# Loading x in four column parts between the first weight units, and the first norm's vector apart from the others

## The chip, the core and the metric

One Trainium2 chip (trn2), one core. The metric is the device time of the whole program in microseconds (us): the median of three executions before the change is 1454.51 us (1451.9 to 1456.7).

## The reference, cut to what matters

One decoder layer on 256 tokens of width 2048, all in f32. What the change touches is the very first step:

```python
h = rms_norm(x, norm_mix[l])
proj = h @ w_in[l]              # columns: q-latent 512 | kv-latent 256 + rope key 64 | SB q, k, v 3 x 1024
# ... MLA attention (softmax, rotary), stick-breaking attention
x = x + concat(rms_norm(o_mla), rms_norm(o_sb)) @ w_out[l]
x = x + memory_cross_attention(rms_norm(x), rms_norm(mem), ...)
x = x + hierarchical_moe(rms_norm(x), ...)   # 32 experts, f32 weights of 12 MB each
y = rms_norm(x)
```

`rms_norm(x, g)` is `x * rsqrt(mean(x*x) + eps) * g`. The kernel multiplies by `g` before the projection and by the factor of each row (the rsqrt) after it, when the accumulated bank is copied out.

## The kernel before, in words

Every engine has one program of its own, run in order, and they meet through semaphores only.

**Weights.** The projections are cut into chunks of 512 output columns (`Q_LAT` = 0, `KV_LAT` = 1 with 320 columns, then `SB_Q`, ...), and each chunk into units of 256 input rows: 8 units for a chunk over D = 2048, 512 KB a unit. `SyncE` (SP) loads unit `u` into slot `u % 4` of the ring `w_raw` (line 312), once `w_split` says that the unit four places back was split (line 304). `ScalarE` (ACT) rounds it to `w_hi` (`rounded`, line 772), which also waits until TensorE has used the unit that held the slot (`w_used`, line 771). `VectorE` (DVE) forms the rest `w_lo = w_raw - w_hi` (`split_w`, line 1066). TensorE (PE) then does twelve matmuls for the unit (lines 408 to 410).

**Activations.** `split_turn` (line 388) transposes x on PE, two 128-column blocks (index k) at a time into one bank of PSUM. ACT makes `a_hi` with the gain as scale (`split_head`, line 798, scale from `g_t`), DVE makes `a_lo` (`split_rest`, line 1077). For the first norm these steps are interleaved with the units: `split_project` on PE (pair kk is turned, then unit kk - 3 is multiplied), `heads_and_units` on ACT, `rests_and_units` on DVE. The 8 pairs use 4 banks of PSUM in turn.

**The start.** SP loads x in two DMAs of 128 rows and waits for both before it issues the first weight unit (lines 299 to 301). ACT issues eight small DMAs of the norm vectors into `g_nat`, two of the positions and one of `g_ffn` (lines 833 to 842), then loads its table. PE waits for the constants and all eight vectors, transposes `g_nat` once (line 448), ACT copies the result to `g_t` (line 845), and PE waits for that copy before it turns x. DVE first computes the rotary angles (lines 1128 to 1149), then begins `rests_and_units`. GpSimd (POOL) writes the inverse frequencies, the identity and the masks.

**The end of the first norm.** ACT, after `heads_and_units("mix")`, squares x for the row factors (`squares_of`, line 778), waits for POOL's pow (`rstd`, lines 1586 and 1587), and only then comes to

```python
            for c in range(Q_LAT, Q_PE):
                rounded(UNIT0[c + 1] + RING)
```

so that units 8 to 11, the first of chunk `KV_LAT`, are rounded behind it. PE comes to `KV_LAT` with `project(c)` right after `split_project`.

After the projections come the attentions, w_out, the attention into memory, the router, and a loop over 32 experts whose weights SP streams from HBM; the first expert's weights are issued when PE has used the units up to `MEM_O` (line 335).

Of the kernel before, what the change touches and what calls it, by code (L numbers as in the profile page):

```python
# [20 lines left out]
ALU = mybir.AluOpType  # L21
ACT = mybir.ActivationFunctionType
AX = mybir.AxisListType.X

P = 128
# [16 lines left out]
SC_SB = float(HD) ** -0.5  # L42
BLK = 3 * P
RING = 4
UK = 2
UN = 512

# [40 lines left out]
def layer(nc, x, mem, positions, norm_mix, w_in, norm_q_lat, w_q_b, norm_kv_lat, w_kv_b,  # L88
# [11 lines left out]
    with ctx:  # L100
# [195 lines left out]

        @block.sync
        def _(sp):
            for t in range(TT):
                sp.dma_start(x_res[:, t, :], x[0, t * P:(t + 1) * P, :]).then_inc(S("x_loaded"), 16)  # L300
            sp.wait_ge(S("x_loaded"), 16 * TT)
            for u, (c, i) in enumerate(UNITS):
                if u >= RING:
                    sp.wait_ge(S("w_split"), u - RING + 1)
                dst = w_raw[:, u % RING, :, 0:chunk_cols(c)]
                (src,) = unit_src(c, i)
                if len(src.shape) == 4:
                    for k in range(UK):
                        sp.dma_start(dst[:, k, :].rearrange("p (h c) -> p h c", h=src.shape[2]),
                                     src[:, k]).then_inc(S(f"w_loaded{u % RING}"), 16)  # L310
                else:
                    sp.dma_start(dst, src).then_inc(S(f"w_loaded{u % RING}"), 16)

            def load_gate_up(e, side, used=None, halves=(0, 1)):

                wg = w_gate[0, e].rearrange("(p k) f -> p (k f)", k=KD)
                wu = w_up[0, e].rearrange("(p k) f -> p (k f)", k=KD)
                half = KD // 2 * FE
                for b in halves:
                    if used is not None:  # L320
                        sp.wait_ge(S(f"gu_used{b}"), used)
                    for m, w in enumerate((wg, wu)):
                        sp.dma_start(gu[side][:, b, m].rearrange("p k f -> p (k f)"),  # L323
                                     w[:, b * half:(b + 1) * half]).then_inc(
                                         S(f"gu_loaded{side}{b}"), 16)

            def load_down(e, used=None):
                wd = w_down[0, e].rearrange("(j p) d -> p j d", p=P)
                for b, dst in enumerate((down0, down1)):
                    if used is not None:  # L330
                        sp.wait_ge(S(f"down_used{b}"), used)
                    sp.dma_start(dst[:, :, :], wd[:, 2 * b:2 * b + 2, :]).then_inc(
                        S(f"down_loaded{b}"), 16)

            sp.wait_ge(S("w_used"), UNIT0[MEM_O])
            sp.wait_ge(S("mem_scores"), MEM_HEADS)

            load_gate_up(0, 0)
            load_down(0)
            sp.wait_ge(S("w_used"), len(UNITS))  # L340
            sp.wait_ge(S("w_split"), len(UNITS))
            load_gate_up(1, 1)
            for e in range(2, AHEAD):
                load_gate_up(e, e % 2, e - 1)
                load_down(e - 1, e - 1)
            load_gate_up(AHEAD, AHEAD % 2, AHEAD - 1, halves=(0,))
            load_down(AHEAD - 1, AHEAD - 1)
            load_gate_up(AHEAD, AHEAD % 2, AHEAD - 1, halves=(1,))
            load_down(AHEAD, AHEAD)
            with sp.Fori(0, (EXPERTS - AHEAD - 1) // 2) as i:  # L350
                for m in range(2):
                    e = 2 * i + AHEAD + 1 + m
                    load_gate_up(e, (AHEAD + 1 + m) % 2, 2 * i + AHEAD + m)
                    load_down(e, 2 * i + AHEAD + 1 + m)
            sp.wait_ge(S("routed"), 1)
            total = sp.value_load(n_iter[0:1, 0:1], min_val=EXPERTS, max_val=MAX_PASSES * EXPERTS)
            with sp.If(total > EXPERTS):

                with sp.Fori(EXPERTS - 1, total - 1, EXPERTS) as before_:
                    with sp.Fori(0, EXPERTS // 2) as i:  # L360
                        for side in range(2):
                            load_gate_up(2 * i + side, side, before_ + 2 * i + side)
                            load_down(2 * i + side, before_ + 2 * i + 1 + side)
            sp.wait_ge(S("gu_used1"), total)
            sp.dma_start(g_fin[:, :], norm_final.rearrange("(a d) -> a d", a=1).to_broadcast([P, D])
                         ).then_inc(S("final_gain_loaded"), 16)
            for t in range(TT):
                for f in range(2):
                    sp.wait_ge(S("final"), 2 * t + f + 1)
                    cols = slice(f * D // 2, (f + 1) * D // 2)  # L370
                    sp.dma_start(out[0, t * P:(t + 1) * P, cols], x_res[:, t, cols]).then_inc(
                        S("stored"), 16)
            sp.wait_ge(S("stored"), 16 * 2 * TT)
# [3 lines left out]
        def _(pe):  # L377
            def split_turn(name, src, k_from=0, k_to=None):

                k0, kn = SPLIT0[name], SPLIT_K[name]  # L380
                for kk in range(k_from // 2, (kn if k_to is None else k_to) // 2):
                    b = k0 // 2 + kk
                    if b >= 4:
                        pe.wait_ge(S("split_lo"), 2 * (b - 4) + 2)
                    for i in range(2):
                        for t in range(TT):
                            k = 2 * kk + i
                            mm = pe.transpose(ps[4 + b % 4][:, i * SEQ + t * P:i * SEQ + (t + 1) * P],  # L388
                                              src[:, t, k * P:(k + 1) * P], ident[:, :])
# [37 lines left out]
            def turn(c):  # L427
# [6 lines left out]
                for b in range(1 if c == KV_LAT else 2):  # L434
# [8 lines left out]
                                              nat[:, j % 2, t, f * P:(f + 1) * P], ident[:, :])  # L443
                    mm.then_inc(S("turned"), 1)

            pe.wait_ge(S("consts"), 1)
            pe.wait_ge(S("gains_loaded"), 8 * 16)
            pe.transpose(ps[0][:, 0:86], g_nat[:, :], ident[0:86, 0:86]).then_inc(S("gains_turned"), 1)
            pe.wait_ge(S("x_loaded"), 16 * TT)
            pe.wait_ge(S("gains_copied"), 1)  # L450
            split_project("mix", x_res, [(Q_LAT, i, 0) for i in range(KD // UK)])
            for c in range(Q_LAT, Q_PE):
                if c > Q_LAT:
                    project(c)
                if SB_Q <= c - 1 < SB_V:
                    turn(c - 1)
# [302 lines left out]
        def _(sc):  # L759
# [70 lines left out]

            xsq = [0]

            for gain, r0, rows in ((norm_mix, 0, 16), (norm_mem_src, 16, 16), (norm_mem_x, 32, 16),
                                   (norm_q_lat, 48, 4), (norm_kv_lat, 52, 2), (norm_mla_out, 54, 8),
                                   (norm_sb_out, 62, 8), (norm_ffn, 70, 16)):
                sc.dma_start(g_nat[r0:r0 + rows, :], gain[0].rearrange("(k p) -> k p", p=P)
                             ).then_inc(S("gains_loaded"), 16)
            for t in range(TT):
                sc.dma_start(pos_i[:, t:t + 1], positions[0, t * P:(t + 1) * P].rearrange(
                    "(p a) -> p a", a=1)).then_inc(S("pos_loaded"), 16)  # L840
            sc.dma_start(g_ffn[:, :], norm_ffn[0].rearrange("(p k) -> p k", k=KD)).then_inc(
                S("ffn_gain_loaded"), 16)
            sc.preload_act_table_set("natural_log_exp_and_others")
            sc.wait_ge(S("gains_turned"), 1)
            sc.activation(g_t[:, :], ps[0][:, 0:86], ACT.Copy).then_inc(S("gains_copied"), 1)
            sc.wait_ge(S("gains_copied"), 1)
            heads_and_units("mix", 0, 0)
            junk = v_mla[:, :, :].rearrange("p t d -> p (t d)")
            squares_of(x_res, SS_X, junk)
            sc.wait_ge(S("rstd"), 1)  # L850
# [200 lines left out]
        def _(ve):  # L1051
# [68 lines left out]
            rt_a = place("rope_tmp", [P, 4, 256], offset=e_at + 80 * 1024)  # L1120


            from math import pi
            import numpy as np
            half = ROPE // 2
# [16 lines left out]
            for cc in (c1, c2, c3):  # L1142
# [4 lines left out]
            link(ve.tensor_tensor(cosv, cosv, turns[:, :, :], ALU.add))  # L1147
            ve.tensor_scalar(rope_cs[:, :, :, :], rope_cs[:, :, :, :], 3.1415925, -3.1415925, ALU.min,
                             ALU.max).then_inc(S("angles"), 1)
            ve.wait_ge(S("gains_copied"), 1)  # L1150
            rests_and_units("mix", 0, 0)
            for c in range(Q_LAT, Q_PE):
                split_w(UNIT0[c + 1] + RING)
                if SB_Q <= c - 1 < SB_V:
# [393 lines left out]
        def _(gp):  # L1548
            steps = [0]

            def link(ins):
# [2 lines left out]
                ins.then_inc(S("gp_step"), 1)  # L1554
                gp.wait_ge(S("gp_step"), steps[0])

            half = ROPE // 2
            for i in range(half):
                ins = gp.memset(small[:, i:i + 1], float(10000.0 ** (-2.0 * i / ROPE)))
            ins.then_inc(S("inv_freq"), 1)  # L1560
            gp.memset(ident[:, :], 0.0)
            gp.memset(ones[:, :], 1.0)
            gp.memset(sb_mask[:, :], 1.0)
            link(gp.memset(mla_mask[:, :], 0.0))
            gp.affine_select(out=ident[:, :], in_=ident[:, :], compare_op=ALU.not_equal, fill=1.0, base=0,
                             pattern=[[-1, P]], channel_multiplier=1)
            gp.affine_select(out=above[:, :], in_=ones[:, :], compare_op=ALU.is_gt, fill=0.0, base=0,
                             pattern=[[-1, P]], channel_multiplier=1)
            for lo in (0, SEQ):
# [87 lines left out]
```

## Time and profile before

| | |
|---|---|
| median of three executions | 1454.51 us (1451.9, 1454.51, 1456.7) |
| span of the profiled execution (first to last instruction) | 1450.0 us |
| the profiled execution's own time | not listed beside its span |
| busy: PE, PEld, DVE, ACT, POOL | 1082.5, 643.9, 540.3, 337.4, 33.2 us |
| DMA over the span | 481.69 MB, mean 332 GB/s |

PE is TensorE's matmuls, PEld its weight loads; SPq and ACTq are the queues of SyncE and ScalarE that issue DMAs. In a row of the timeline the time in brackets is how long the engine sat idle before, and what ended it. The page's slices show PE nearly full for the first third of the span and the DMA engines full for the last 60%.

### The profile page before, as it was taken

To read this page: it belongs to the slowest core of one execution; us is meant where nothing else is said; L and a number is where in the kernel's file an instruction comes from. 1 tells how busy PE (TensorE), PEld (TensorE's weight loads), DVE (VectorE), ACT (ScalarE), POOL (GpSimd) and SP (SyncE) were. 2 spreads that over 40 slices of the span, in tenths; PEclk is the share of its full clock that TensorE was granted. 3 is DMA by queue.
4 is the path that set the end of the run, shared out by engine and by line. 5 is a ranking of instruction groups with operands and counts; after the bars stand their busy time and mean duration, and the time that the engine had idled before them with its cause. 6 is when DMAs were issued, how large, how long until landed. Compare 5 with 4: busy or idle time off the path is not lost.

```text
span 1450.0 us, 21354 instructions
## 1 busy us (share of the span) xinstructions
PE 1082.5 (75%) x8717; PEld 643.9 (44%) x8717; DVE 540.3 (37%) x1120; ACT 337.4 (23%) x609; POOL 33.2 (2%) x90
## 2 busy tenths in 40 slices
PE   6999988998998968667656666667656665666665
PEld 5888867777887733222222222223222222222222
DVE  5444556565564433322222222222222222222323
ACT  5554455565444230100000000000000000000002
POOL 1000000110001000000000000000000000000000
PEclk9999999999999988988888888788888898788977
DMA  6766743222655789999999999999999999999996
GB/s 212 268 190 189 185 134 116 87 88 93 209 182 176 322 350 423 428 425 426 428 427 427 423 428 427 427 424 427 427 427 425 426 428 427 427 424 427 427 427 259
DMA packets 85379, 481.69 MB, mean 332 GB/s; under 512 B 10262, under 2 KB 20636, under 8 KB 51932
## 3 DMA queue, kind: packets, MB, share of 16 engines
q1 hardware_dynamic: 84272, 478.70, 82.5%
q10 hardware_dynamic: 876, 2.15, 0.4%
q0 software_dynamic: 192, 0.31, 0.2%
q8 instruction: 25, 0.41, 0.1%
q14 instruction: 14, 0.11, 0.0%
HBM read 479.04 MB, written 2.10 MB: 332 GB/s over the span
## 4 chain that ended last, share of the span: by engine, by line
DMA 47%; PE 41%; ACT 3%; DVE 3%; SPq 3%; issue 1%; POOL 0%; DVEq 0%; ACTq 0%; POOLq 0%
DMA gu<-in_w_up 29%; DMA down<-in_w_down 17%; PE ps L408 8%; PE ps L410 8%; PE ps L409 8%; PE ps L684 5%; PE ps L731 5%; SPq L323 2%; PE ps L665 2%; PE ps L388 1%; PE ps L674 1%; DVE w_lo L1066 1%; PE ps L483 1%; ACT x_slots L1015 1%; DMA x_res<-in_x 1%
## 5 line engine op out<-in xcount | busy, mean ns | idle before, releaser
L684 PE MATMUL ps<-gu,xe 128*32 128x256 f32 x4096 | 317.9, 479 | 232.8 <-DMA gu<-in_w_up 231.8
L684 PEld LDWEIGHTS ps<-gu,xe 128*32 128x32 f32 x4096 | 153.9, 137 | 417.7 <-DMA gu<-in_w_up 279.0
L1461 DVE TENSOR_TENSOR x_res<-ps,x_res 128x512 f32<-128x512 f32 x248 | 153.9, 683 | 406.9 <-PE ps L694 406.9
L408 PE MATMUL ps<-w_hi,a_hi 128*128 128x512 f32 (+1 forms) x552 | 220.5, 399 | 8.6 <-DVE w_lo L1066 3.6
L409 PE MATMUL ps<-w_lo,a_hi 128*128 128x512 f32 (+1 forms) x552 | 215.9, 391 | 0.0
L1066 DVE TENSOR_TENSOR w_lo<-w_raw,w_hi 128x1024 fp32r<-128x1024 f32 (+1 forms) x138 | 163.9, 1200 | 132.0 <-ACT w_hi L772 131.1
L410 PE MATMUL ps<-w_hi,a_lo 128*128 128x512 f32 (+1 forms) x520 | 202.7, 390 | 0.0
L772 ACT ACTIVATE w_hi<-w_raw 128x1024 fp32r<-128x1024 f32 (+1 forms) x138 | 141.8, 1038 | 150.6 <-PE ps L410 142.8
L1022 ACT ACTIVATE sg<-ps 128x128 f32<-128x128 f32 x32 | 8.9, 278 | 625.8 <-PE ps L684 625.8
L731 PE MATMUL ps<-down,turned 128*32 128x512 f32 x1024 | 122.8, 611 | 31.6 <-ACT turned L1028 24.4
L408 PEld LDWEIGHTS ps<-w_hi,a_hi 128*128 128x128 f32 x552 | 106.0, 192 | 29.8 <-ACT w_hi L772 2.5
L409 PEld LDWEIGHTS ps<-w_lo,a_hi 128*128 128x128 f32 x552 | 106.0, 192 | 19.6
L410 PEld LDWEIGHTS ps<-w_hi,a_lo 128*128 128x128 f32 x520 | 99.2, 191 | 20.4
L694 PE MATMUL ps<-y_sb,turned 32*128 32x512 f32 x512 | 75.7, 645 | 25.1 <-ACT y_sb L1031 24.3
L731 PEld LDWEIGHTS ps<-down,turned 128*32 128x32 f32 x1024 | 29.6, 111 | 102.5 <-issue 80.0
L1491 DVE TENSOR_TENSOR act<-sg,ps 128x128 f32<-128x128 f32 x32 | 9.2, 288 | 166.3 <-ACT sg L1022 166.3
L665 PE MATMUL ps<-h_nat,hot 128*32 128x512 f32 x528 | 64.0, 603 | 3.1 <-DVE hot L1443 3.1
L1452 DVE TENSOR_TENSOR xe<-ps,g_ffn 128x128 f32<-128x128 f32 x132 | 29.1, 283 | 82.2 <-PE ps L674 82.2
L694 PEld LDWEIGHTS ps<-y_sb,turned 32*128 32x128 f32 x512 | 21.9, 184 | 68.6 <-issue 40.5
L1031 ACT ACTIVATE y_sb<-ps 128x512 f32<-128x512 f32 x32 | 19.1, 597 | 135.3 <-PE ps L731 135.3
L674 PE MATMUL ps<-ident,x_slots 128*128 128x128 f32 x132 | 21.6, 286 | 23.7 <-ACT x_slots L1015 23.7
L1077 DVE SCALAR_TENSOR_TENSOR a_lo<-ps,g_t,a_hi 128x256 fp32r<-128x256 f32 x70 | 29.5, 477 | 22.8 <-ACT a_hi L798 22.3
(233 smaller groups left out, 685.7 us busy)
## 6 DMA issues: line engine op xcount, KB each, us to landing
gu<-in_w_gate SPq DMA_DIRECT2D x64, 2048.0 KB, 31.7
gu<-in_w_up SPq DMA_DIRECT2D x64, 2048.0 KB, 36.1
down<-in_w_down SPq DMA_DIRECT2D x64, 2048.0 KB, 24.6
w_raw<-in_w_in SPq DMA_DIRECT2D x56, 512.0 KB, 4.0
w_raw<-in_w_out SPq DMA_DIRECT2D x32, 512.0 KB, 4.2
w_raw<-in_w_mem_kv SPq DMA_DIRECT2D x16, 512.0 KB, 3.7
w_raw<-in_w_mem_q SPq DMA_DIRECT2D x8, 512.0 KB, 3.4
w_raw<-in_w_mem_o SPq DMA_DIRECT2D x8, 512.0 KB, 4.4
```

The source lines that it names most:

```text
L408: pe.matmul(acc[t][:, 0:n], xh, wh, start=(k == 0), stop=False)
L409: pe.matmul(acc[t][:, 0:n], xh, wl, start=False, stop=False)
L410: mm = pe.matmul(acc[t][:, 0:n], xl, wh, start=False, stop=(k == kn - 1))
L665: mm = pe.matmul(ps[4][g * SLOTS:(g + 1) * SLOTS, :], hot[:, t, :], h_nat[:, t, 4 * g:4 * g + 4, :].rearrange("p k d -> p (k d)"), start=( ...
L674: mm = pe.transpose(ps[4][:, j * P:(j + 1) * P], x_slots[:, j * P:(j + 1) * P], ident[:, :])
L684: mm = pe.matmul(ps[5][j * SLOTS:(j + 1) * SLOTS, 0:2 * P].rearrange("s (m f) -> s m f", m=2), xe[:, k, :], gu[side][:, b, :, kk, j * P:(j ...
L694: return pe.matmul(ps[g][:, :], turned_6[rows, t, :], y_sb[rows, :], start=True, stop=True)
L731: mm = pe.matmul(ps[7][g * SLOTS:(g + 1) * SLOTS, :], act_t[:, j * SLOTS:(j + 1) * SLOTS], w[:, jj, g * UN:(g + 1) * UN], start=(j == 0), ...
L772: sc.activation(w_hi[:, u % RING, :, 0:n], w_raw[:, u % RING, :, 0:n], ACT.Copy).then_inc(S("w_rounded"), 1)
L1066: ve.tensor_tensor(w_lo[:, u % RING, :, 0:n], w_raw[:, u % RING, :, 0:n], w_hi[:, u % RING, :, 0:n], ALU.subtract).then_inc(S("w_split"), 1)
L1077: ve.scalar_tensor_tensor(out=lo[:, a0 + k, :], in0=ps[4 + b % 4][:, i * SEQ:(i + 1) * SEQ], scalar=1.0 if g0 is None else g_t[:, g0 + k:g ...
L1461: ins = ve.tensor_tensor(xs, ps[g][:, :], xs, ALU.add)
```

## The change

Four things. (1) SP no longer waits for x: it issues x in four DMAs of 512 columns (512 KB each), each followed by one weight unit, and PE waits for a part (`x_loaded0` to `x_loaded3`) ahead of the pair of blocks that needs it. (2) ACT issues only the DMA of `norm_mix`; PE transposes those 16 rows into bank 2, ACT copies 16 columns of `g_t`, and x is turned without waiting for that copy. (3) The ten other small DMAs are issued by SP ahead of unit 4. PE transposes all 86 rows of `g_nat` after `split_project`, into bank 3; ACT copies columns 16 to 85 after `heads_and_units`, ahead of `squares_of`; PE waits for that copy ahead of chunk `KV_LAT`. (4) DVE computes the rotary angles after `rests_and_units`, and POOL makes the identity first.

```diff
@@ -42,6 +42,7 @@
 SC_SB = float(HD) ** -0.5
 BLK = 3 * P
 RING = 4
+X_PARTS = 4
 UK = 2
 UN = 512
 
@@ -296,10 +297,26 @@
 
         @block.sync
         def _(sp):
-            for t in range(TT):
-                sp.dma_start(x_res[:, t, :], x[0, t * P:(t + 1) * P, :]).then_inc(S("x_loaded"), 16)
-            sp.wait_ge(S("x_loaded"), 16 * TT)
+            def load_small():
+
+                for gain, r0, rows in ((norm_mem_src, 16, 16), (norm_mem_x, 32, 16),
+                                       (norm_q_lat, 48, 4), (norm_kv_lat, 52, 2), (norm_mla_out, 54, 8),
+                                       (norm_sb_out, 62, 8), (norm_ffn, 70, 16)):
+                    sp.dma_start(g_nat[r0:r0 + rows, :], gain[0].rearrange("(k p) -> k p", p=P)
+                                 ).then_inc(S("gains_loaded"), 16)
+                for t in range(TT):
+                    sp.dma_start(pos_i[:, t:t + 1], positions[0, t * P:(t + 1) * P].rearrange(
+                        "(p a) -> p a", a=1)).then_inc(S("pos_loaded"), 16)
+                sp.dma_start(g_ffn[:, :], norm_ffn[0].rearrange("(p k) -> p k", k=KD)).then_inc(
+                    S("ffn_gain_loaded"), 16)
+
             for u, (c, i) in enumerate(UNITS):
+                if u < X_PARTS:
+                    cols = slice(u * D // X_PARTS, (u + 1) * D // X_PARTS)
+                    sp.dma_start(x_res[:, :, cols], x[0, :, cols].rearrange("(t p) d -> p t d", p=P)
+                                 ).then_inc(S(f"x_loaded{u}"), 16)
+                if u == RING:
+                    load_small()
                 if u >= RING:
                     sp.wait_ge(S("w_split"), u - RING + 1)
                 dst = w_raw[:, u % RING, :, 0:chunk_cols(c)]
@@ -382,6 +399,8 @@
                     b = k0 // 2 + kk
                     if b >= 4:
                         pe.wait_ge(S("split_lo"), 2 * (b - 4) + 2)
+                    if name == "mix" and kk % 2 == 0:
+                        pe.wait_ge(S(f"x_loaded{kk // 2}"), 16)
                     for i in range(2):
                         for t in range(TT):
                             k = 2 * kk + i
@@ -443,14 +462,18 @@
                                               nat[:, j % 2, t, f * P:(f + 1) * P], ident[:, :])
                     mm.then_inc(S("turned"), 1)
 
+            pe.wait_ge(S("ident_made"), 1)
+            pe.wait_ge(S("mix_gain_loaded"), 16)
+            pe.transpose(ps[2][:, 0:16], g_nat[0:16, :], ident[0:16, 0:16]).then_inc(
+                S("gains_turned"), 1)
+            split_project("mix", x_res, [(Q_LAT, i, 0) for i in range(KD // UK)])
+            pe.wait_ge(S("gains_loaded"), 7 * 16)
+            pe.transpose(ps[3][:, 0:86], g_nat[:, :], ident[0:86, 0:86]).then_inc(S("gains_turned"), 1)
             pe.wait_ge(S("consts"), 1)
-            pe.wait_ge(S("gains_loaded"), 8 * 16)
-            pe.transpose(ps[0][:, 0:86], g_nat[:, :], ident[0:86, 0:86]).then_inc(S("gains_turned"), 1)
-            pe.wait_ge(S("x_loaded"), 16 * TT)
-            pe.wait_ge(S("gains_copied"), 1)
-            split_project("mix", x_res, [(Q_LAT, i, 0) for i in range(KD // UK)])
             for c in range(Q_LAT, Q_PE):
                 if c > Q_LAT:
+                    if c == KV_LAT:
+                        pe.wait_ge(S("gains_copied"), 2)
                     project(c)
                 if SB_Q <= c - 1 < SB_V:
                     turn(c - 1)
@@ -830,21 +853,16 @@
 
             xsq = [0]
 
-            for gain, r0, rows in ((norm_mix, 0, 16), (norm_mem_src, 16, 16), (norm_mem_x, 32, 16),
-                                   (norm_q_lat, 48, 4), (norm_kv_lat, 52, 2), (norm_mla_out, 54, 8),
-                                   (norm_sb_out, 62, 8), (norm_ffn, 70, 16)):
-                sc.dma_start(g_nat[r0:r0 + rows, :], gain[0].rearrange("(k p) -> k p", p=P)
-                             ).then_inc(S("gains_loaded"), 16)
-            for t in range(TT):
-                sc.dma_start(pos_i[:, t:t + 1], positions[0, t * P:(t + 1) * P].rearrange(
-                    "(p a) -> p a", a=1)).then_inc(S("pos_loaded"), 16)
-            sc.dma_start(g_ffn[:, :], norm_ffn[0].rearrange("(p k) -> p k", k=KD)).then_inc(
-                S("ffn_gain_loaded"), 16)
+            sc.dma_start(g_nat[0:16, :], norm_mix[0].rearrange("(k p) -> k p", p=P)).then_inc(
+                S("mix_gain_loaded"), 16)
             sc.preload_act_table_set("natural_log_exp_and_others")
             sc.wait_ge(S("gains_turned"), 1)
-            sc.activation(g_t[:, :], ps[0][:, 0:86], ACT.Copy).then_inc(S("gains_copied"), 1)
+            sc.activation(g_t[:, 0:16], ps[2][:, 0:16], ACT.Copy).then_inc(S("gains_copied"), 1)
             sc.wait_ge(S("gains_copied"), 1)
             heads_and_units("mix", 0, 0)
+            sc.wait_ge(S("gains_turned"), 2)
+            sc.activation(g_t[:, 16:86], ps[3][:, 16:86], ACT.Copy).then_inc(S("gains_copied"), 1)
+            sc.wait_ge(S("gains_copied"), 2)
             junk = v_mla[:, :, :].rearrange("p t d -> p (t d)")
             squares_of(x_res, SS_X, junk)
             sc.wait_ge(S("rstd"), 1)
@@ -1120,6 +1138,8 @@
             rt_a = place("rope_tmp", [P, 4, 256], offset=e_at + 80 * 1024)
 
 
+            ve.wait_ge(S("gains_copied"), 1)
+            rests_and_units("mix", 0, 0)
             from math import pi
             import numpy as np
             half = ROPE // 2
@@ -1147,8 +1167,6 @@
             link(ve.tensor_tensor(cosv, cosv, turns[:, :, :], ALU.add))
             ve.tensor_scalar(rope_cs[:, :, :, :], rope_cs[:, :, :, :], 3.1415925, -3.1415925, ALU.min,
                              ALU.max).then_inc(S("angles"), 1)
-            ve.wait_ge(S("gains_copied"), 1)
-            rests_and_units("mix", 0, 0)
             for c in range(Q_LAT, Q_PE):
                 split_w(UNIT0[c + 1] + RING)
                 if SB_Q <= c - 1 < SB_V:
@@ -1554,16 +1572,16 @@
                 ins.then_inc(S("gp_step"), 1)
                 gp.wait_ge(S("gp_step"), steps[0])
 
+            link(gp.memset(ident[:, :], 0.0))
+            gp.affine_select(out=ident[:, :], in_=ident[:, :], compare_op=ALU.not_equal, fill=1.0, base=0,
+                             pattern=[[-1, P]], channel_multiplier=1).then_inc(S("ident_made"), 1)
             half = ROPE // 2
             for i in range(half):
                 ins = gp.memset(small[:, i:i + 1], float(10000.0 ** (-2.0 * i / ROPE)))
             ins.then_inc(S("inv_freq"), 1)
-            gp.memset(ident[:, :], 0.0)
             gp.memset(ones[:, :], 1.0)
             gp.memset(sb_mask[:, :], 1.0)
             link(gp.memset(mla_mask[:, :], 0.0))
-            gp.affine_select(out=ident[:, :], in_=ident[:, :], compare_op=ALU.not_equal, fill=1.0, base=0,
-                             pattern=[[-1, P]], channel_multiplier=1)
             gp.affine_select(out=above[:, :], in_=ones[:, :], compare_op=ALU.is_gt, fill=0.0, base=0,
                              pattern=[[-1, P]], channel_multiplier=1)
             for lo in (0, SEQ):
```

## Rows read from the trace of the kernel before

**Rows 1.** The page's part 4: shares of the chain that ended last, by engine.

```profile
DMA 47%; PE 41%; ACT 3%; DVE 3%; SPq 3%; issue 1%; POOL 0%; DVEq 0%; ACTq 0%; POOLq 0%
```

**Rows 2.** Windows: stretch, its length, busy (instructions) by engine, PEclk, DMA share, GB/s.

```profile
19.15:40.91 21.76, 21.76 (x104) 18.02 (x103) 12.33 (x18) 13.15 (x19) 0.91 (x2) 1.00 0.47 140
40.91:54.99 14.08, 14.08 (x98) 14.07 (x96) 6.50 (x8) 9.37 (x14) 0.90 (x2) 1.00 0.76 246
54.99:189.20 134.21, 134.21 (x610) 111.38 (x609) 66.38 (x70) 61.28 (x67) 0.88 (x2) 1.00 0.71 208
189.20:195.50 6.30, 2.05 (x15) 1.43 (x13) 3.25 (x7) 4.51 (x9) 0.00 (x0) 0.84 0.68 199
195.50:200.00 4.50, 4.48 (x11) 3.53 (x12) 0.75 (x2) 0.00 (x0) 0.00 (x0) 0.50 0.00 0
508.00:1450.00 942.00, 609.47 (x6424) 251.80 (x6423) 261.80 (x699) 79.64 (x155) 2.40 (x6) 0.85 0.99 417
```

**Rows 3.** Timeline to the first matmul: start, duration, engine, line, operation, idle before.

```profile
0.80 0.43 ACTq L836 DMA_DIRECT2D g_nat<-in_norm_mix  x1
0.81 0.88 SPq L300 DMA_DIRECT2D x_res<-in_x  x2
...
3.85 0.32 ACTq L836 DMA_DIRECT2D g_nat<-in_norm_ffn  x1
...
8.71 49.26 SPq L312 DMA_DIRECT2D w_raw<-in_w_in  x24
...
9.24 0.38 PE L448 MATMUL ps<-ident,g_nat 86*128 86x86 f32 x1 [9.24 <-DMA g_nat<-in_norm_ffn]
...
9.65 0.24 ACT L845 ACTIVATE g_t<-ps 128x86 f32<-128x86 f32 x1 [2.73 <-PE ps L448]
...
10.04 3.65 PE L388 MATMUL ps<-ident,x_res 128*128 128x128 f32 x16 [0.42 <-ACT g_t L845]
...
11.23 0.84 ACT L798 ACTIVATE a_hi<-ps,g_t 128x256 fp32r<-128x256 f32 x2 [1.33 <-PE ps L388]
...
12.71 1.06 ACT L772 ACTIVATE w_hi<-w_raw 128x1024 fp32r<-128x1024 f32 x1 [0.64 <-DMA w_raw<-in_w_in]
...
13.80 1.23 DVE L1066 TENSOR_TENSOR w_lo<-w_raw,w_hi 128x1024 fp32r<-128x1024 f32 x1 [0.66 <-ACT w_hi L772]
...
15.17 0.77 PE L408 MATMUL ps<-w_hi,a_hi 128*128 128x512 f32 x1 [1.48 <-DVE w_lo L1066]
```

**Rows 4.** Landing times of DMAs into x_res, then of the first five into w_raw.

```profile
DMA to landing us min/median/max: 5.0/6.2/7.4
...
DMA to landing us min/median/max: 3.6/4.9/6.5
```

**Rows 5.** DMA queues: ACT's in 2 to 3 and 3 to 4; all in 12 to 13.5.

```profile
q10 hardware_dynamic: 8, 0.00, 1.4%
...
q10 hardware_dynamic: 24, 0.00, 2.2%
...
DMA packets 315, 0.61 MB, mean 406 GB/s; under 512 B 18, under 2 KB 18, under 8 KB 315
```

**Rows 6.** Timeline of ACT, then of DVE, behind the first norm's last weight unit.

```profile
31.88 1.91 ACT L778 ACTIVATE v_mla<-x_res 128x2048 f32<-128x2048 f32 x1
...
37.07 2.12 ACT L772 ACTIVATE w_hi<-w_raw 128x640 fp32r<-128x640 f32 x3 [1.16 <-issue]
...
37.84 2.29 DVE L1066 TENSOR_TENSOR w_lo<-w_raw,w_hi 128x640 fp32r<-128x640 f32 x3 [4.60 <-ACT w_hi L772]
```

**Rows 7.** The chain that ended last, start to 60 us: start, share, what.

```profile
18.92 0.43 PE ps L410
...
20.55 0.23 PE ps L408
```

**Rows 8.** Timeline of DVE: first and last instruction of the rotary angles.

```profile
9.55 0.17 DVE L1130 CAST small<-pos_i 128x2 f32<-128x2 int32 x1 [9.55 <-DMA pos_i<-in_positions]
...
12.13 0.23 DVE L1148 TENSOR_SCALAR rope_cs<-rope_cs 128x128 f32<-128x128 f32 x1
```

## The prediction

> **What bounds the kernel now.** I read the shares of the chain first: DMA 47%, PE 41% [rows 1]. The windows then show where each of the two holds. From 508 us to the end the DMA engines are 0.99 busy at 417 GB/s and PE is only the consumer; from 19 to 189 us PE is busy in every microsecond (21.76 of 21.76, 14.08 of 14.08, 134.21 of 134.21) while DVE and ACT have room [rows 2]. The stream of expert weights starts when PE has used the units up to `MEM_O`. So a microsecond won or lost on PE ahead of 189 us moves everything behind it, and reaches the end whole. The timeline of the first 15 us shows the third piece: the first multiplication starts only at 15.17 [rows 3]. The change works on that piece, and on the joint between the first and the second chunk at 40.91, where the windows show PE without a gap [rows 2].
>
> **Part 1, the start.** Before, two x DMAs go out at 0.81, SP waits until 8.71, and only then issues weight unit 0; it is rounded at 12.71, split at 13.80, and used at 15.17 [rows 3]. Four weight DMAs issued together from 8.71 give the pace of 512 KB loads in one queue: the first lands in about 4.0 us (rounding starts at 12.71), and at 406 GB/s [rows 5] each next one 1.3 us later (0.524 MB / 406 GB/s); the slowest of the first five took 6.5 us [rows 4]. With eight loads of this size issued from 0.81 on, part 0 of x lands at 4.8, unit 0 at 6.1, part 1 at 7.4, unit 1 at 8.7, then 10.0, 11.3, 12.6 and 13.9. The two x DMAs of 1 MB in 5.0 to 7.4 us [rows 4] fit this.
>
> PE needed 3.65 us for 16 transposes, and the first `a_hi` came 1.19 us after their start (10.04 to 11.23) [rows 3]. Turning pairs 0 and 1 from 4.8 takes 1.8 us; pairs 2 and 3 wait for part 1 at 7.4 and end near 9.2. Beside it: `a_hi` at 6.0, 0.8 us long; `w_hi` 6.8 to 7.9; `w_lo` 1.23 us, to 9.1. Both ways lead to a first matmul at about **9.2 instead of 15.17: 6.0 us won**. Later parts don't bind: part 2 (10.0) is wanted after unit 0, which at the start's pace ends near 14, and unit 4 is wanted after 22, while SP, with eight large issues and ten small ones at 0.3 to 0.45 us each [rows 3], is free near 9, when unit 0 is split and unit 4 may be issued anyway. The small loads' packets stand in the same queue ahead of unit 4 and cost it under 1 us (the old queue moved them beside 2 MB of x), which that slack hides.
>
> The gain vector of the first norm must be in `g_t` at 6.0. Its DMA goes out at 0.80 as before. ACT's queue moved 8 and 24 packets in the stretches 2 to 3 and 3 to 4 [rows 5], more than its 16 rows, so it lands by about 4.5; transpose and copy take 0.4 and 0.24 (9.24, 9.65) [rows 3], ready near 5.2. Bound on the bad side: as slow as the `norm_ffn` vector, issued 3.85 and awaited until 9.24, 5.4 us [rows 3]: lands at 6.2, first matmul at 10.7, only 4.5 us won. On the good side the parts could land 0.8 us earlier (no unit waited for before them): 6.8 won. I take 6.0, as the packets are seen early.
>
> The identity comes earlier on POOL; by then nothing waits for it. The wait of PE for `g_t` (0.42) goes too [rows 3], inside the times above.
>
> **A page against the split.** In the 12 to 13.5 stretch, 512 KB loads ran at 406 GB/s [rows 5]. The Trainium skill (DMA: Bandwidth & Descriptors, section Bandwidth) advises batches of 1 MiB or more and lists 341 GB/s at that size, so halves of it would be slower. By 341 GB/s a load would follow each 1.5 us, part 1 would land at 7.9, and the gain at the start would be an estimated 5.5 instead of 6.0. The trace disagrees where several loads queue up, so I stay with 6.0.
>
> **Part 2, the second copy of the gains.** Here the cost is. PE transposes the rest of `g_nat` only after unit 7, its last of `Q_LAT`. ACT stands at this transposition before `squares_of`, and behind `squares_of` and POOL's pow it has to round units 8 to 11. Before, ACT began to square at 31.88, right behind unit 7's rounding, and reached unit 8 at 37.07, DVE split it at 37.84 [rows 6]: 2.3 us ahead of PE, which came at 40.91 [rows 2]. All of that was under PE's units 5 to 7. Now it can start only when PE has ended unit 7. The serial chain, with PE idle: transpose until ACT may read, 0.4 (9.24 to 9.65); copy 0.24 and ACT's wait for its own copy, together 0.35; squares, pow and waits, 31.88 to 37.07, 5.19; rounding until split begins, 0.77 [rows 6]; `w_lo` of 640 columns 0.76 (2.29 / 3) and 0.14 to PE (13.80 + 1.23 to 15.17) [rows 3], 0.9. **Sum 7.6 us.** Queued behind ACT's wait are, besides unit 8, units 9 to 11 and the copy of `c_q`; for unit 8 PE waits at once.
>
> `Q_LAT` now ends at 40.9 - 6.0 = 34.9, so `KV_LAT` starts at 42.5 instead of 40.9: **+1.6 us**.
>
> **Part 3, the clock after the hole.** The column for the clock shows 0.84 over the hole of 189 to 195.5, where PE was busy 2.05 of 6.30 us, and 0.50 (1.2 instead of 2.4 GHz) in the 4.5 us after it [rows 2]. At the start a matmul of 512 columns stood at 0.43 until 18.92, at 0.23 from 20.55 [rows 7]. A hole of 7.6 us with nearly nothing in it should bring the low level too. At the start it lasted 4.2 us (15.17 to 19.35), after 195.5 4.5 us. Work at the low level yields 0.23/0.43 of the time: 4.2 us lose **2.0 us**. Bounds: nothing, if the clock stays (no row shows it over such a hole), and 2.1. I take 2.0. At the start itself the low level lasts as before; transposes begin closer to the matmuls, which could give back up to 0.9, taken as 0.
>
> Behind the hole supply doesn't bind again: ACT rounds units 9 to 11 at 0.7 each, DVE splits at 0.76, PE takes 1.76 (14.08 / 8) at full clock; ACT then has 2.8 us of `c_q`, and comes to unit 12 near 46.5, wanted near 51. ACT was busy 9.37 and DVE 6.50 of 14.08 us there [rows 2].
>
> **Part 4, the rotary angles.** 2.8 us of DVE (9.55 to 12.36) [rows 8] move from ahead of the first `a_lo`, where they cost about 0.2, to behind unit 7's split. DVE was busy 12.33 of 21.76 us there [rows 2] and is now idle until unit 8 is rounded: cost nothing. If that cover were gone, they would cost their 2.8.
>
> **Sum.** -6.0 + 7.6 + 2.0 = +3.6 us on the profiled execution's span of 1450.0: 1453.6. Its own time isn't listed; the median of the runs is 4.5 above the span and I keep that distance: **1458.1 us, 0.25% more**. Under 0.3% (4.4 us) a measurement of this kernel can't tell a difference from none.
>
> **Rivals.**
> - *Late gain vector* (slower by over 0.3%). The one small DMA shares the engines with x; `a_hi` of pair 0 waits for it. From 0.8 us later than my 4.5 + 0.6 it decides, each microsecond one to one. At 6.2 the start wins 4.5: +5.1, 1459.6. For it: 5.4 us of `norm_ffn`. Against it: the packets of 2 to 4 us. A page bears on it: the Trainium skill (DMA: Bandwidth & Descriptors, section Issuing engines are not separate DMA queues) says that DMAs from different engines interleave on the same 16. Chance 0.20.
> - *Parts land together.* If the eight loads share the engines, part 0 lands near 12 and the change doesn't do what it says: first matmul at about 15 as before, and the hole remains: +9.6, 1464.1. Against it: the first weight unit landed in 4.0 with three behind it [rows 3]. Chance 0.05.
> - *No hole* (faster by over 0.3%): the squares and unit 8 hide under PE, and all 6.0 stays: 1448.5. For it: 2.3 us of lead at 37.84 before. Against it: the order of ACT's program puts 5.19 us behind PE's last unit. Partial form: clock not lowered and start at 6.8: -6.8 + 7.6 = +0.8, 1455.3, which is no change. Chance of the full form 0.06.
> - The forecast with its bounds, the partial form included: 0.69, of which 0.05 lies above +4.4 us and 0.02 is a favourable drift of the long DMA stage beyond the bound.
>
> So faster 0.08, within 0.3% 0.62, slower 0.30. The range reaches from the partial form less 2.3 us (half the spread of the three runs, 2.4) to the late gain vector plus the same: 1453.0 to 1462.0.
>
> **What would show it.** In the profile after: first matmul of L408's successor near 9.2 (part 1); a PE idle time of about 7.6 us ahead of the first 320-column matmul, near 35 to 42.5, released by DVE's `w_lo`, and ACT idle about 9 us ahead of the second copy to `g_t` (part 2); clock 0.50 and doubled spacing for some 4 us behind it (part 3); the rotary angles inside that stretch (part 4). Wrong it would be if the first squares began before PE's unit 7 ends, if the hole is under 6 us, or if the DMA stage doesn't start later by what `KV_LAT` lost.

## The result and the profile after

The changed kernel takes 1460.73 us (median of 20 runs, 1453.34 to 1463.76), the kernel before 1455.14 us (20 runs): ratio 1.004, 95% interval 1.0028 to 1.0051. That is 5.6 us, or 0.4% slower. The prediction had said 1458.1 us, 0.25% slower, with 0.30 for slower than 0.3%. The profiled execution has a span of 1459.0 us.

Start of the changed kernel, from its timeline (columns as in [rows 3], whose steps these lines answer):

```profile
2.69 0.25 PE L467 MATMUL ps<-ident,g_nat 16*128 16x16 f32 x1 [2.69 <-DMA g_nat<-in_norm_mix]
...
2.98 0.18 ACT L860 ACTIVATE g_t<-ps 128x16 f32<-128x16 f32 x1 [0.41 <-PE ps L467]
...
5.04 1.97 PE L407 MATMUL ps<-ident,x_res 128*128 128x128 f32 x8 [2.10 <-DMA x_res<-in_x]
...
6.99 1.06 ACT L795 ACTIVATE w_hi<-w_raw 128x1024 fp32r<-128x1024 f32 x1
...
9.10 1.97 PE L407 MATMUL ps<-ident,x_res 128*128 128x128 f32 x8 [2.08 <-DMA x_res<-in_x]
...
10.72 0.77 PE L427 MATMUL ps<-w_hi,a_hi 128*128 128x512 f32 x1
```

The gain vector is there at 2.69, long before it is needed. Part 0 of x is there at 5.04, but part 1 only at 9.10, not 7.4; PE stands 2.08 us for it, and the first multiplication starts at 10.72, 4.45 us sooner than before [rows 3].

Then the joint between the first two chunks, in the timelines of ACT and of PE, which answer to [rows 6]:

```profile
35.54 0.23 ACT L864 ACTIVATE g_t<-ps 128x70 f32<-128x70 f32 x1 [9.22 <-PE ps L471]
35.80 1.91 ACT L801 ACTIVATE v_mla<-x_res 128x2048 f32<-128x2048 f32 x1
...
41.00 2.62 ACT L795 ACTIVATE w_hi<-w_raw 128x640 fp32r<-128x640 f32 x4 [1.16 <-issue]
```

```profile
42.74 0.61 PE L427 MATMUL ps<-w_hi,a_hi 128*128 128x320 f32 x1 [7.23 <-DVE w_lo L1084]
...
46.34 0.36 PE L428 MATMUL ps<-w_lo,a_hi 128*128 128x320 f32 x1
```

ACT stands 9.22 us idle for the second transposition (PE does it at 35.27), and only then squares x; unit 8 is rounded at 41.00, 5.2 us after the squares began, and PE stands 7.23 us. The windows show the three stretches (columns as in [rows 2]):

```profile
12.14:35.10 22.96, 22.96 (x110) 18.98 (x109) 15.01 (x31) 9.92 (x17) 0.00 (x0) 1.00 0.62 192
35.50:42.74 7.24, 0.01 (x2) 0.04 (x1) 0.98 (x2) 5.98 (x8) 0.91 (x2) 0.78 0.00 0
42.74:46.40 3.66, 3.66 (x14) 3.66 (x15) 2.06 (x3) 3.47 (x9) 0.04 (x1) 0.50 0.72 200
46.40:58.56 12.16, 12.16 (x84) 12.16 (x84) 6.15 (x7) 6.14 (x7) 0.85 (x2) 1.00 0.80 244
58.56:192.80 134.24, 134.24 (x611) 111.38 (x610) 65.99 (x70) 61.28 (x67) 0.88 (x2) 1.00 0.71 208
```

The third number from the end of a line is the granted clock. PE is full, then empty, then full at half the clock (0.50, 1.2 GHz), then full at 2.4 GHz. The third chunk starts at 58.56 instead of 54.99: 3.57 us later, where the prediction's sum is +3.6. The stretch to 192.80 is as long as before (134.24 against 134.21 [rows 2]), so nothing is made up in it.

### The profile page after: what moved, and what is told of

Its sections match the earlier page's. It is cut to its first block, busy times and chain, and to the rows that moved or that the text cites. A ratio compares the mean times of both kernels' runs of the same rounds, so it can differ in the third digit from the quotient of the medians.

```text
span 1459.0 us, 21361 instructions
## 1 busy us (share of the span) xinstructions
PE 1086.1 (74%) x8718; PEld 646.0 (44%) x8718; DVE 540.5 (37%) x1120; ACT 337.8 (23%) x610; POOL 33.4 (2%) x90
## 4 chain that ended last, share of the span: by engine, by line
DMA 46%; PE 39%; SPq 4%; ACT 3%; DVE 3%; issue 1%; POOL 0%; DVEq 0%; ACTq 0%; POOLq 0%
DMA gu<-in_w_up 27%; DMA down<-in_w_down 19%; PE ps L427 8%; PE ps L429 8%; PE ps L428 8%; PE ps L754 4%; PE ps L707 4%; SPq L340 3%; PE ps L688 2%; PE ps L407 1%; PE ps L506 1%; PE ps L697 1%; PE ps L461 1%; ACT h_nat L1021 1%; ACT x_slots L1033 0%
```

## Experiments

Eleven further runs; each ratio is to the kernel before on the same chip. Theory H: the loss is the hole and the low clock behind it, and all comes from the place of the second gain transposition. Rivals: the loss is in the loading itself (L), or comes far behind (C).

**Gains turned midway.** The hole is taken away, all else stays (diffs here are cut to the lines that matter).

```diff
-            split_project("mix", x_res, [...])
-            pe.wait_ge(S("gains_loaded"), 7 * 16)
-            pe.transpose(ps[3][:, 0:86], g_nat[:, :], ident[0:86, 0:86]).then_inc(S("gains_turned"), 1)
+            split_project("mix", x_res, [...], midway=8)    # the same two lines, ahead of unit 5
```

> The changed kernel, with TensorE's second transposition of the gains moved from behind unit 7 to ahead of unit 5 of the first chunk (ScalarE's copy stays where it is). Theory H (the hole): the squares and units 8 to 11 hide again, KV_LAT starts at about 35.2 us with no idle time, the low clock of 42.7 to 46.3 is gone; 9.3 us less than the changed kernel as profiled (7.2 + 0.3 + 1.7), 5 to 6 us under the kernel before: ratio 0.996. Rival L (the loading: split x, small vectors on the weights' queue): the loss stays, ratio 1.003 or more. Rival C (an extra of about 2 us far behind the hole comes with the change itself): ratio 0.9975.

Measured: 1451.67 us, ratio 0.9972 (0.9954 to 0.999); a repeat on another occasion 1450.79 us, 0.9978 (0.9958 to 0.9997). Its ACT and then its PE:

```profile
27.33 0.23 ACT L866 ACTIVATE g_t<-ps 128x70 f32<-128x70 f32 x1 [1.05 <-PE ps L443]
27.59 1.92 ACT L803 ACTIVATE v_mla<-x_res 128x2048 f32<-128x2048 f32 x1
```

```profile
35.13 0.39 PE L429 MATMUL ps<-w_hi,a_lo 128*128 128x512 f32 x1
35.36 0.30 PE L427 MATMUL ps<-w_hi,a_hi 128*128 128x320 f32 x1
```

No gap between the last matmul of 512 columns and the first of 320. With the same loading it is faster than the changed kernel on the same chip, by 9.4 us between the medians (1461.12, under Controls below) and by 7.3 us between the two ratios: rival L falls. It gains 3 to 4 us on the kernel before; the 5 to 6 expected lie within the interval, but both runs came out below them; the third chunk starts 5.6 us sooner (49.43), in the repeat 4.2 (50.79).

> The kernel with the gains turned midway again, on the same chip as the version with unit 0 sooner. Ratio to before 0.997; KV_LAT at 34.8 to 36.3 us, by how soon the clock rises in unit 0.

**The kernel before, held.** Only the hole is put in.

```diff
+            sc.wait_ge(S("w_used"), 8)
             squares_of(x_res, SS_X, junk)
```

> The kernel before, with ScalarE waiting until TensorE has used unit 7 before it squares x; all else as before. Theory H: a hole of 6.9 us (squares to first matmul) ahead of KV_LAT and the low clock behind it, 1.7: +8.6 us, ratio 1.006. Rival L: a held ScalarE costs less than 2 us, ratio under 1.0015, since the loss was in the loading.

Measured: 1462.97 us, ratio 1.0046 (1.0031 to 1.0061). Its PE:

```profile
47.46 0.60 PE L408 MATMUL ps<-w_hi,a_hi 128*128 128x320 f32 x1 [6.97 <-DVE w_lo L1067]
```

The idle time is the 6.9 us expected, the third chunk starts at 63.82, 8.8 us later than in the first trace (8.6 expected). The ratio is worth 6.7 us, under the 1.006 expected but with it inside the interval. One wait, with the old loading, brings the hole and a loss as large as that of the whole change (the intervals overlap): H is shown from both sides.

**Squares first.** The changed kernel with ACT's copy moved, PE's program untouched.

```diff
-            sc.wait_ge(S("gains_turned"), 2)     # and the copy to g_t[:, 16:86], ahead of squares_of
             squares_of(x_res, SS_X, junk)
             sc.wait_ge(S("rstd"), 1)
+            rounded(UNIT0[KV_LAT] + RING - 1)
+            sc.wait_ge(S("gains_turned"), 2)     # and the copy, here
```

> The changed kernel with ScalarE's second copy of the gains moved behind the squares, the row factors and the rounding of units 8 to 10; TensorE's program is untouched. Theory H: only ScalarE's order made the hole; KV_LAT waits for the transposition and the copy alone, about 0.7 us, starts at 35.9 to 36.4, clock stays high; 5 us under the kernel before, ratio 0.9965 to 0.9975. If TensorE's late transposition were the cost, the hole would stay over 3 us.

Measured: 1451.46 us, ratio 0.9981 (0.9964 to 0.9997). Its PE around the joint:

```profile
36.23 0.24 PE L471 MATMUL ps<-ident,g_nat 86*128 86x86 f32 x1
36.84 0.38 PE L427 MATMUL ps<-w_hi,a_hi 128*128 128x320 f32 x1 [0.36 <-issue]
```

The late transposition costs 0.6 us by itself. ACT's order made the hole: a wait for PE's last unit stood ahead of 5.2 us of work that had been hidden under PE. Its start of `KV_LAT`, 36.84, is later than the 35.9 to 36.4 expected, because the fast spacing of the matmuls began later in unit 0 (14.56 instead of 12.14). The gain, 2.8 us by the ratio, is under the 5 us expected (0.9965 to 0.9975, partly inside the interval), though clear of none.

**The hole filled.** 28 matmuls without use in the hole of the changed kernel.

```diff
+            for _ in range(28):
+                pe.matmul(ps[7][:, :], a_hi[:, 0, 0:P], a_hi[:, 0:2, :]..., start=True, stop=True)
```

> The changed kernel, with 28 further matmuls of 512 columns on TensorE behind its second transposition of the gains; they write a bank that nobody reads (work added, nothing used). They fill 6.4 us of the hole of 7.2. Theory H with its clock term: the idle time falls under 1 us, KV_LAT still starts at about 42.7, but at the high clock: 1.7 us less than the changed kernel, ratio to before 1.0028. If the clock term is nothing: no gain, ratio 1.004. If the filling keeps the clock from falling later too, up to 2 us more.

Measured: 1457.54 us, ratio 1.0014 (1.0001 to 1.0027).

```profile
36.26 6.64 PE L473 MATMUL ps<-a_hi 128*128 128x512 f32 x28
43.71 0.38 PE L427 MATMUL ps<-w_hi,a_hi 128*128 128x320 f32 x1 [0.81 <-DVE w_lo L1087]
```

`KV_LAT` to the third chunk takes 14.15 us (43.71 to 57.86), as before (14.08 [rows 2]), against 15.82 in the changed kernel. So the clock term is **1.7 us**. `KV_LAT` starts at 43.71 and not at the 42.7 expected, since the matmuls of unit 0 became fast later in this execution too (14.54), so only 0.7 us of it are left at the third chunk. The ratios point the same way (1.0014 against 1.0022 for the control on that chip), but their intervals overlap; the stretch carries this, not the total.

**The parts alone.** SP's and PE's side of the loading, on the kernel before; the small loads, the single transposition and the angles stay.

```diff
-            for t in range(TT):              # two x DMAs, and the wait for both
+                if u < X_PARTS:              # in the loop over units: 512 columns of x, then the unit
```

> The kernel before with only SyncE's and TensorE's side of the loading changed: x in four column parts, each followed by a weight unit; all small loads stay on ScalarE's queue ahead, one transposition of all gains, rotary angles first. Theory: the wait for the last small vector (9.2 us) then bounds the start: first matmul at 13 to 14 instead of 15.17, 1.2 to 2 us won; ratio 0.999. Rival: the parts alone bring the whole early start: first matmul at 10.7, ratio 0.997.

Measured: 1456.97 us, ratio 1.002 (1.001 to 1.003). I had expected a gain, and it is a loss. The lines of its start:

```profile
10.34 0.38 PE L452 MATMUL ps<-ident,g_nat 86*128 86x86 f32 x1 [10.34 <-DMA g_nat<-in_norm_ffn]
...
11.94 0.17 DVE L1133 CAST small<-pos_i 128x2 f32<-128x2 int32 x1 [11.94 <-DMA pos_i<-in_positions]
...
15.45 1.22 DVE L1069 TENSOR_TENSOR w_lo<-w_raw,w_hi 128x1024 fp32r<-128x1024 f32 x1
```

With eight loads of 512 KB issued beside them (4 MB, where x alone was 2), the last small vector comes at 10.34 instead of 9.24 and the positions at 11.94 instead of 9.55 [rows 3, 8]; the angles follow up to 14.8 and hold VectorE's first rest and split, and the first matmul is at 16.81. So the parts alone bring nothing here; they bring something together with the small loads moved away and the angles moved behind. This run doesn't separate these two; the next one does for the angles.

**Angles first.** Gains midway, but the rotary angles back ahead of `rests_and_units`.

```diff
+            # the angles, from the wait for pos_loaded on
             ve.wait_ge(S("gains_copied"), 1)
             rests_and_units("mix", 0, 0)
-            # the angles
```

> The kernel with the gains turned midway, with the rotary angles back ahead of VectorE's first rests and units, while the positions are still loaded by SyncE behind four parts and four units. Theory: the positions land near 16 us, the angles take 2.8, then rest and unit 0's split 2.1: first matmul at about 21 instead of 10.6, ratio 1.003 to 1.005. If the order of the angles were worth only the 0.2 us of part 4 of the prediction, no difference to the version it is made from.

Measured: 1463.77 us, ratio 1.0075 (1.0049 to 1.01).

```profile
16.80 0.17 DVE L1150 CAST small<-pos_i 128x2 f32<-128x2 int32 x1 [16.80 <-DMA pos_i<-in_positions]
```

```profile
21.67 0.77 PE L427 MATMUL ps<-w_hi,a_hi 128*128 128x512 f32 x1 [10.48 <-DVE w_lo L1086]
```

The first matmul is at 21.67, near the 21 expected, but the ratio lies above the expected 1.003 to 1.005, nearly all of its interval too. (The profiled execution is the fastest of the six, 1455.66; the other five took 1463.2 to 1465.8.) Without the edit that I costed at nothing, the first matmul comes 11 us later, once the positions are loaded behind the rest.

**Unit 0 sooner.** Gains midway, and the unit lag on PE is one pair instead of three.

```diff
-            split_project("mix", x_res, [...], midway=8)
+            split_project("mix", x_res, [...], lag=1, midway=7)
```

> The kernel with the gains turned midway (the hole closed), and on TensorE unit 0 multiplied behind pair 1 instead of behind pair 3, so that it needs part 0 of x and unit 0 only. Theory: the start is bound by part 1 of x, which landed at 8.9 to 9.1 us, not by unit 0, which was split at 9.3; first matmul at about 9.4 instead of 10.6, KV_LAT 1 us earlier; ratio to before 0.996 to 0.997. Rival: the later units are short of data (unit 2 landed at 13.1, unit 3 at 15.9), the 1.2 us are given back in waits ahead of units 2 and 3, KV_LAT starts at 35 as without it.

Measured: 1457.01 us, ratio 1.0023 (1.0005 to 1.004): a miss on both counts. The first matmul came at 9.50, as said, but `KV_LAT` at 40.20:

```profile
33.26 1.92 ACT L803 ACTIVATE v_mla<-x_res 128x2048 f32<-128x2048 f32 x1
```

```profile
40.20 0.39 PE L427 MATMUL ps<-w_hi,a_hi 128*128 128x320 f32 x1 [2.68 <-DVE w_lo L1086]
```

The units are hardly short of data (one wait in `Q_LAT`, 0.24 us at unit 7), and still there is no gain: with the last pairs of x turned two units later, ACT ends `heads_and_units` later, squares x at 33.26 instead of 27.59, and the same serial chain is in the open again, for 2.68 us. The short gap costs more than itself: behind it the granted clock is 0.50 again, and `KV_LAT` takes 15.69 us (40.20 to 55.89) instead of 14.08, a loss of 1.6 us, as large as behind the hole of 7.2 (the last section has the lines).

**Controls and a pure shift.** The first traces also differ behind the third chunk. These are the windows from its start to the issue of the first expert's weights (SP's queue), one line for each trace. The two of the kernel before:

```profile
54.99:504.80 449.81, 425.94 (x2043) 350.16 (x2041) 248.87 (x371) 226.24 (x406) 25.09 (x32) 0.98 0.53 171
```

```profile
54.41:507.18 452.77, 429.36 (x2043) 352.73 (x2041) 248.67 (x371) 226.37 (x406) 25.06 (x32) 0.97 0.52 170
```

The two of the changed kernel:

```profile
58.56:511.52 452.96, 429.04 (x2043) 352.58 (x2041) 248.63 (x371) 226.32 (x406) 25.07 (x32) 0.97 0.53 170
```

```profile
58.17:511.26 453.09, 429.20 (x2043) 352.63 (x2041) 248.51 (x371) 226.27 (x406) 25.05 (x32) 0.97 0.52 170
```

The two with the gains midway:

```profile
49.43:497.96 448.53, 424.88 (x2043) 349.73 (x2041) 248.51 (x371) 226.27 (x406) 25.07 (x32) 0.98 0.53 172
```

```profile
50.79:506.15 455.36, 431.06 (x2043) 354.06 (x2041) 249.40 (x372) 226.81 (x407) 25.08 (x32) 0.96 0.52 169
```

> The changed kernel itself again, as a control on the same chip: ratio 1.004 as recorded. Its trace is for the stretches behind 190 us: if the 1.6 us more between 190 and 246 us and the 1.5 us more up to 505 us belong to the change, they stand here too; if they are stretches of low clock that fall by chance, they stand elsewhere or are missing, by 1 us or more.

> The kernel before itself again, one look for its trace, as a control. In the first trace the stretch from the start of the third chunk (54.99 us) to the first expert's weights (504.80) took 449.8 us, and in both traces of the changed kernel 453.0. If where the clock falls is fixed by when the gaps come, this trace has 449.8 within 0.5 and its low stretches at the same places; if it is chance, it differs by 1 us or more.

The changed kernel's control gave 1461.12 us, ratio 1.0022 (1.0004 to 1.0039), and a second trace like its first. The kernel before gave 1456.16 in its single execution and a second trace unlike its first: 452.77, as long as the changed kernel's. The shifted kernel is the kernel before with 16 unused matmuls ahead of `KV_LAT`:

> The kernel before with 16 further matmuls of 512 columns on TensorE ahead of KV_LAT (their result is not used): a pure shift of everything behind by 3.6 us, at the high clock, as large as the changed kernel's shift at the third chunk. Theory S (the shift decides in which later gaps the clock falls): the stretch to the first expert's weights grows from 449.8 to about 453, low stretches near 240 and 285 to 295 us as in the changed kernel; ratio 1.003 to 1.004. Rival A (the extra comes from something else in the change): 449.8 stays, shift 3.6 only, ratio 1.0025 or less.

Its third chunk starts at 58.07, its stretch is 452.75 long, as theory S said; but since the control of the kernel before has that length without any shift, this doesn't speak for S. Its time is 1459.46 us, ratio 1.0019 (0.9999 to 1.0039). That fits a pure delay of PE's program that reaches the end (3.6 us would be 1.0025), but the interval reaches down to none, so it isn't shown by this run. Rival C falls for the 3 us that the first two traces differed by here: they need nothing of the change. The stretch varies between executions of one and the same kernel, by up to 6.8 us (448.53 and 455.36, on two chips), in step with the mean granted clock (0.98 and 0.96).

## Why the prediction was right, and where its sizes were off

- **Part 1, the start: the mechanism right, the first matmul mis-sized.** 4.45 us won instead of 6.0. The step that was off is "each next one 1.3 us later": part 1 landed at 9.1, not 7.4, and unit 1 near 10.4, not 8.7. Two windows show why:

```profile
0.80:5.04 4.24, 0.25 (x1) 0.17 (x1) 0.00 (x0) 1.47 (x2) 3.81 (x43) 1.00 0.63 191
5.04:9.10 4.06, 1.97 (x9) 1.57 (x9) 1.89 (x3) 2.52 (x5) 0.10 (x1) 1.00 1.01 305
```

When part 0 (0.52 MB) had landed, 0.81 MB had been moved (4.24 us at 191 GB/s), so data of the loads behind it had gone beside it; and from there to the landing of part 1 the rate was 305 GB/s with the engines full, not 406. The number in flight alone doesn't lower the rate: from 9 to 13 us the same queue moved 397 to 410 GB/s. Nor is it the queue of the small loads: with the parts alone they are in ACT's, and 6 to 8 us show 257 GB/s against 246 here. The cause of the lower rate stays open. With the figure of the Trainium skill for loads of 1 MB (DMA: Bandwidth & Descriptors, section Bandwidth) the prediction had an estimate of 7.9 for part 1, which is nearer to 9.1, but no run here tells the size of a load from its place among the others.

- **Given back in unit 0.** The slow spacing after the first matmul (0.43 us, then 0.23) lasted 1.4 us (10.72 to 12.14) instead of the 4.2 taken; I had allowed such a gain up to 0.9 and set it to zero. It made up for 1.2 of the missing 1.55 us: `Q_LAT` gave way to the transposition at 35.27, against 34.9. This term is a draw: with the gains midway the fast spacing began at 12.44 in one execution and at 15.12 in the other, and `KV_LAT` at 35.36 and 36.71. That this is the low clock is an inference from the spacing, as in the prediction: the column of the granted clock shows 1.00 in this stretch, and shows the low level only behind the later gaps, where the spacing is the same 0.43.
- **The late vector** did not come: 2.69 us. Neither did the parts land together; the part of that rival that holds is the slower part 1.
- **Part 2, the hole:** `KV_LAT` starts 1.8 us later, 1.6 were said; the serial chain is as summed, 7.47 us from the transposition on (35.27 to 42.74) against 7.6, and the squares to unit 8 are 5.20 against 5.19. Squares first and the held kernel show that ACT's order is the cause.
- **Part 3, the clock:** 1.7 us instead of 2.0, by the filled hole; the low level lasted 3.6 us (42.74 to 46.34) instead of 4.2. The size varies: behind the 6.97 us of the held kernel it lasted 4.9 us (47.46 to 52.38), and `KV_LAT` took 16.36 us, 2.3 more than 14.08.
- **Part 4, the angles:** the CAST runs at 27.49, behind unit 7's split, the last of the angles at 30.07, and DVE is then idle until 41.76. Nothing, as said, though they ran ahead of the hole and not inside it, where the prediction looked for them. What was left out is that the move is a condition of the new loading (11 us without it).
- **The sum** at the third chunk is +3.57 against +3.6: -5.64 for `Q_LAT` (35.27 against 40.91), +7.47 for the hole, +1.74 for the clock (15.82 against 14.08). That it agrees to 0.03 is luck, since 1.55 us too little at the start and 1.2 us given back nearly cancel; the second traces give +3.76 (58.17 against 54.41). At the end the 20 runs show +5.6 (interval 4.1 to 7.4), the control +3.2 (1.0022; 0.6 to 5.7); only the second holds 3.6. The difference of the two spans, 9.0 us, is not the change's: 3.15 of it arise between 55 and 512 us, where the first trace of the kernel before was 3 us shorter than its second, and 2.3 in the stage of the experts, where the traces of all these kernels lie between 944.9 and 950.4 us. Whether the excess of 5.6 over 3.6 is chance or a small effect of the shift stays open; the pure shift of 3.6 (1.0019, 0.9999 to 1.0039) allows both. So the sign that the DMA stage starts later by what `KV_LAT` lost is met only roughly: 6.7 us later in the first traces (511.52 against 504.80), 4.1 in the second (511.26 against 507.18).
- **The classes.** The time lies in the stated range, but beyond the 0.3% that the prediction thought likeliest (0.62). The 0.30 for more stood mostly for a late gain vector and for parts that land together, and neither came. And "can't tell a difference from none" under 0.3% was too wide: the interval of the 20 runs is 0.12% to either side.

## What to carry to other kernels

When a wait is added to an engine's program, look at what is queued behind it there, not at what the waited-for thing costs: a transposition of 0.24 us opened a hole of 7.2 us, since 5.2 us of hidden work stood behind it in order. Loads that were split to start work sooner paid here only once the small loads and the chain on them were moved too, and a part landed later than its place in the queue and the full rate say, as data of the loads behind it moved beside it. A short gap of PE can cost more than its length, by the low clock behind it (2.68 us, and 1.6 more). A difference of a few us in the spans of two traces should be set beside a second trace of each before it is explained.

## What the runs showed of the hardware

The granted clock fell in the same gaps of PE in some executions and not in others. In windows of 4 us, first of the first, then of the second trace of the kernel before, in which PE stands idle in the same places (1.50 us ahead of a transposition of `mem_sb`):

```profile
234.00:238.00 4.00, 2.50 (x13) 1.84 (x14) 3.40 (x11) 3.94 (x12) 0.00 (x0) 1.00 0.40 133
238.00:242.00 4.00, 4.00 (x22) 3.30 (x21) 3.91 (x10) 1.76 (x6) 1.02 (x1) 1.00 0.01 4
```

```profile
234.00:238.00 4.00, 2.50 (x12) 1.99 (x11) 3.93 (x12) 3.94 (x12) 0.00 (x0) 0.82 0.39 133
238.00:242.00 4.00, 4.00 (x17) 3.19 (x16) 2.71 (x6) 0.50 (x3) 1.01 (x1) 0.75 0.01 4
```

PE was busy 2.50 us in the first window of both, yet the clock is 1.00 in one and 0.82 in the other, and then 22 matmuls in 4 us against 17. Over the stretch of 450 us two executions of one kernel differ by up to 6.8 us, more than this change, at a mean clock of 0.98 and 0.96.

The low level need not begin in the gap. In the kernel with unit 0 sooner PE stands 2.68 us ahead of `KV_LAT` at a clock of 1.00; the first matmuls behind it follow each other by 0.15 us, and only from 40.95 to 44.15 by 0.27, at 0.50:

```profile
37.40:40.20 2.80, 0.12 (x1) 0.03 (x1) 0.97 (x2) 1.74 (x3) 0.90 (x2) 1.00 0.00 0
40.95:44.15 3.20, 3.20 (x13) 3.20 (x13) 1.31 (x2) 3.10 (x8) 0.24 (x2) 0.50 0.88 269
```

In the hole of the changed kernel it begins inside (0.78 over 35.50 to 42.74). The time lost behind the gap was 1.6 us here and 1.7 us there, so it doesn't go by the length of the gap.
